# Another order at attention's end, w_out's chunks loaded ahead, and other steps for the evictions and the refill of the first down projection

## The reference

```python
h = rms_norm(x, norm_mix)
q, k, v, cb, cc, cu = split(h @ w_in)          # 8 heads of 64; 512 conv channels
q, k = rms_norm(q, q_norm), rms_norm(k, k_norm)     # per head
z = q @ k.T / 8                                # s < t only
a = sigmoid(z) * prod(1 - sigmoid(z_tj) for s < j < t)
attn = a @ v
conv = cb * conv3(cc * cu)                     # causal, depthwise
x = x + concat(attn, conv) @ w_out
h = rms_norm(x, norm_ffn)
x = x + (silu(h @ w_gate) * (h @ w_up)) @ w_down    # d_ff 2816
```

## Time and profile before

| | |
|---|---|
| median of 3 runs | 2509.22 us |
| the profiled execution | 2507.85 us, of which 2506.0 span |
| PE busy | 2435.7 us (97%), DVE 57%, POOL 53%, ACT 47% |
| 330 to 1005 us, attention | PE busy 660.52 of 675 |
| 1005 to 1055 us, its end and mix's opening | PE busy 36.56 of 50, mean clock 0.90 |
| 1055 to 1210 us, rest of mix | PE busy 155.00 of 155 |
| 1210 to 1650 us, gate and up, first half | PE busy 436.78 of 440 |
| 1650 to 1868 us, down, first half | PE busy 209.27 of 218 |
| 1868 to 2285 us, gate and up, second half | PE busy 414.51 of 417 |
| 2285 to 2506 us, down, second half | PE busy 214.74 of 221 |

### The profile page before, as it was taken

One profiled execution on the slowest core, in us unless ns is written; L12 is line 12 of the kernel. 1 busy time (PEld: TensorE's weight loads), 2 busy tenths in 40 slices (PEclk: granted clock), 3 DMA queues, 4 the chain that ended last, 5 costly groups with the idle time before them and its releaser, 6 DMA issues.

```text
span 2506.0 us, 34829 instructions
## 1 busy us (share of the span) xinstructions
PE 2435.7 (97%) x12008; PEld 2031.9 (81%) x12008; DVE 1417.4 (57%) x1461; ACT 1168.2 (47%) x1864; POOL 1324.2 (53%) x918
## 2 busy tenths in 40 slices
PE   8999989999899999799999999999999999999999
PEld 6788878888788888688788888878778888888887
DVE  4444367777777777435665555535645555553343
ACT  3322267777777777323433333334443333333433
POOL 1455367778678687203655445324875455451253
PEclk9999999999999999999999999999999999999999
DMA  5989855443534532444432332467553322325766
GB/s 185 300 287 289 270 173 126 135 109 99 159 96 113 149 100 73 134 143 168 143 115 87 113 103 92 152 225 249 184 187 101 121 90 98 126 76 188 227 208 203
DMA packets 337225, 388.17 MB, mean 155 GB/s; under 512 B 21440, under 2 KB 242752, under 8 KB 334784
## 3 DMA queue, kind: packets, MB, share of 16 engines
q1 hardware_dynamic: 337088, 386.49, 49.1%
HBM read 263.20 MB, written 123.21 MB: 154 GB/s over the span
## 4 chain that ended last, share of the span: by engine, by line
PE 87%; POOL 3%; DVE 3%; DMA 2%; issue 2%; SPq 1%; ACT 1%; DVEq 0%; ACTq 0%; POOLq 0%
PE lay_ps L2447 11%; PE lay_ps L2449 11%; PE lay_ps L2451 11%; PE lay_ps L102 9%; PE lay_ps L103 9%; PE lay_ps L104 9%; PE lay_ps L2477 5%; PE lay_ps L2479 4%; PE lay_ps L2478 4%; PE lay_ps L1281 4%; PE lay_ps L1288 2%; PE lay_ps L1265 2%; PE lay_ps L1287 2%; PE lay_ps L1266 2%; POOL lay_A L2356 1%
## 5 line engine op out<-in xcount | busy, mean ns | idle before, releaser
L2356 POOL TENSOR_TENSOR lay_A<-lay_raw,lay_A 128x512 fp32r<-128x512 f32 x264 | 364.3, 1392 | 378.5 <-ACT lay_A L1988 378.5
L2447 PE MATMUL lay_ps<-lay_B,lay_A 128*128 128x512 f32 x1232 | 480.0, 390 | 2.7 <-ACT lay_s L2010 2.7
L2451 PE MATMUL lay_ps<-lay_B,lay_A 128*128 128x512 f32 x1232 | 479.5, 389 | 0.0
L2449 PE MATMUL lay_ps<-lay_B,lay_A 128*128 128x512 f32 x1232 | 479.5, 389 | 0.0
L1132 DVE TENSOR_TENSOR_SCAN lay_stick<-lay_ps,lay_stick 128x128 f32<-128x128 f32 (+5 forms) x192 | 331.2, 1725 | 146.7 <-ACT lay_ps L1033 136.1
L1185 POOL TENSOR_TENSOR lay_a<-lay_a,lay_stick 128x128 f32<-128x128 f32 (+5 forms) x192 | 281.4, 1471 | 144.1 <-DVE lay_stick L1132 137.5
L1988 ACT ACTIVATE lay_A<-lay_raw 128x512 fp32r<-128x512 f32 x264 | 162.2, 627 | 300.0 <-DMA lay_raw<-in_w_gate 119.6
L2032 ACT ACTIVATE lay_A<-lay_A_over 128x1024 fp32r<-128x1024 f32 x154 | 163.1, 1060 | 251.9 <-PE lay_ps L2479 225.9
L2223 DVE TENSOR_TENSOR lay_A<-lay_A_over,lay_A 128x1024 fp32r<-128x1024 f32 x104 | 155.1, 1494 | 211.1 <-ACT lay_A L2032 211.0
L2447 PEld LDWEIGHTS lay_ps<-lay_B,lay_A 128*128 128x128 f32 x1232 | 231.5, 188 | 51.6 <-POOL lay_A L2356 2.9
L2449 PEld LDWEIGHTS lay_ps<-lay_B,lay_A 128*128 128x128 f32 x1232 | 231.5, 188 | 48.0
(11 more groups left out here) (143 smaller groups left out, 5033.0 us busy)
## 6 DMA issues: line engine op xcount, KB each, us to landing
hid_ops<-lay_s SPq DMA_DIRECT2D x154, 256.0 KB, 2.1
lay_A_over<-hid_ops SPq DMA_DIRECT2D x154, 256.0 KB, 3.0
lay_w_stage<-in_w_in SPq DMA_DIRECT2D x48, 512.0 KB, 4.9
lay_raw<-in_w_gate SPq DMA_DIRECT2D x22, 1024.0 KB, 5.7
lay_raw<-in_w_up SPq DMA_DIRECT2D x22, 1024.0 KB, 8.1
lay_A_over<-wd_ops SPq DMA_DIRECT2D x88, 256.0 KB, 3.6
lay_A_over<-in_w_down SPq DMA_DIRECT2D x66, 256.0 KB, 4.1
lay_wd_raw<-in_w_down SPq DMA_DIRECT2D x11, 1024.0 KB, 6.7
```

The lines of the kernel that those rows point to most:

```text
L2356: nc.gpsimd.tensor_tensor(A[:, j, p, 1, :, :], operand(j, p), A[:, j, p, 0, :, :].bitcast(F32), ALU.subtract).then_inc(lo_done, 1)
L2447: nc.tensor.matmul(ps[:, b, :], A[:, j, p, 0, k, :], B[p][:, 0, k, :], start=first_mm, stop=False, skip_group_check=True)
L2449: nc.tensor.matmul(ps[:, b, :], A[:, j, p, 0, k, :], B[p][:, 1, k, :], start=False, stop=False, skip_group_check=True)
L2451: mm = nc.tensor.matmul(ps[:, b, :], A[:, j, p, 1, k, :], B[p][:, 0, k, :], start=False, stop=last_mm, skip_group_check=True)
```

## The change

At attention's end the units' last pieces, mix's splits, the weights' splits and the chunks stand in another order on ACT, DVE and PE. DVE takes over POOL's two splits of the first tiles, and its scan of unit 47 stands behind the low part of unit 44. Six chunks of w_out are loaded ahead instead of two; chunks c = 2 to 5 have buffers of their own in the part of `aT` that no group uses. The order of chunks becomes 0, 1, 2, 4, 6, 3, 7, 5 for tiles 0 and 1.

In the down projection the two halves share the new places of evictions, of `y_to_21` and `y_to_22`, of `store_z` 0 and `load_z` 1, and the new order of raw buffers (with it the four first loads wait for product 6). In the first half `load_b` issues two per step at e = 10 to 17, and the b pieces have other steps. At the second half's start ACT makes casts 2 to 7 before its round and 8 to 13 inside it, each with the wait that it needs.

```diff
+        mix["w_early"] = []
+        for part in ("aT_hi", "aT_lo"):
+            m.offset = m.starts[part] + 4 * GW * (KB + KB // 2)
+            mix["w_early"] += [m.at(f"m_w_early_{part}{i}", [P, D]) for i in range(2)]
...
             store_o(PAIRS - 1, NG - 3)
-            mix["load_w"](2)
-            mix["load_w"](3)
+            mix["load_w"](6)
+            mix["load_w"](7)
...
             pairs(act, body)
-            for i in range(2):
-                mix["mix_split"](i)
-            for n in range(NU - LAG, NU):
-                aT_part(PAIRS - 1, n)
-                if opens[n - 1]:
-                    o_part(PAIRS - 1, units[n - 1][0] - 1)
-                mix["w_part"](n - NU + LAG)
+            mix["mix_split"](0)
+            aT_part(PAIRS - 1, NU - 3)
+            mix["w_part"](0)
+            mix["mix_split"](1)
+            aT_part(PAIRS - 1, NU - 2)
+            o_part(PAIRS - 1, NG - 2)
+            aT_part(PAIRS - 1, NU - 1)
+            mix["w_part"](1)
+            mix["w_part"](2)
             o_part(PAIRS - 1, NG - 1)
...
-                    running_product(p, n)
+                    late = is_last(p) and n == NU - 1
+                    if not late:
+                        running_product(p, n)
...
                         aT_part(p, n - LAG)
+                    if late:
+                        running_product(p, n)
 
             pairs(dve, body)
-            for n in range(NU - LAG, NU):
-                aT_part(PAIRS - 1, n)
-                if opens[n - 1]:
-                    o_part(PAIRS - 1, units[n - 1][0] - 1)
-                if n > NU - LAG:
-                    mix["w_part"](n - NU + LAG - 1)
+            aT_part(PAIRS - 1, NU - 3)
+            mix["mix_split"](0)
+            mix["w_part"](0)
+            mix["mix_split"](1)
+            aT_part(PAIRS - 1, NU - 2)
+            aT_part(PAIRS - 1, NU - 1)
+            o_part(PAIRS - 1, NG - 2)
+            mix["w_part"](1)
             o_part(PAIRS - 1, NG - 1)
...
             pairs(pool, body)
-            for i in range(2):
-                mix["first_split"](i)
...
             pairs(pe, body)
-            for n in range(NU - LAG, NU):
-                if opens[n]:
-                    upper_values(PAIRS - 1, units[n][0] - 1)
-                transposes(PAIRS - 1, n)
-                if opens[n]:
-                    lower_values(PAIRS - 1, units[n][0] - 1)
-                if n > NU - LAG:
-                    for i in range(2):
-                        mix["chunk"](i, n - NU + LAG - 1)
+            transposes(PAIRS - 1, NU - 3)
+            upper_values(PAIRS - 1, NG - 2)
+            transposes(PAIRS - 1, NU - 2)
+            lower_values(PAIRS - 1, NG - 2)
+            transposes(PAIRS - 1, NU - 1)
+            for i in range(2):
+                mix["chunk"](i, 0)
             lower_values(PAIRS - 1, NG - 1)
+            for i in range(2):
+                mix["chunk"](i, 1)
...
+    CHUNKS = (0, 1, 2, 4, 6, 3, 7, 5)
...
-        def load_w(k):
-            wait(sp, w_lo_done, k - 1)
-            sp.dma_start(w_stage[:, k % 2, :], w_out[k * P:(k + 1) * P, :]).then_inc(w_in_sem[k % 2], DMA)
+        def load_w(c):
+            k = CHUNKS[c]
+            if c > 5:
+                sp.wait_ge(w_lo_done, c - 5)
+            sp.dma_start(w_raw(c), w_out[k * P:(k + 1) * P, :]).then_inc(w_loaded(c), DMA)
...
             sp.wait_ge(att.z_full, att.first_head_scored)
-            load_w(0)
-            load_w(1)
+            for c in range(6):
+                load_w(c)
...
-T_AT, B_HI_AT, B_LO_AT = 26, 31, 34
+T_AT = (19, 21, 23, 25, 27, 29, 31, 37, 39, 41, 43, 45, 51, 53, 55, 57)
+B_HI_AT, B_LO_AT = (27, 39, 48, 59), (28, 40, 58, 66)
...
-        op_raw = [flat(Af, j, p) for j, p in ((GATE, P5), (GATE, P6), (UP, P5), (UP, P6))]
+        op_raw = [flat(Af, j, p) for j, p in ((UP, P6), (GATE, P5), (GATE, P6), (UP, P5))]
...
-        hi_at, lo_at = ([first + 7 * m // 5 for m in range(28)] for first in (B_HI_AT, B_LO_AT))
+        hi_at = [first + 9 * i // 7 for first in B_HI_AT for i in range(7)]
+        lo_at = [first + 9 * i // 7 for first in B_LO_AT for i in range(7)]
...
-                    if G == 0 and e - 10 in range(4 * GT):
-                        load_b(e - 10)
-                    if e == ENDS[D2] + 10:
+                    if G == 0 and e - 10 in range(2 * GT):
+                        load_b(2 * (e - 10))
+                        load_b(2 * (e - 10) + 1)
+                    if e == ENDS[D2] + 13:
                         store_z(G, 0)
-                    if e == ENDS[D2] + 13:
+                    if e == ENDS[D2] + 15:
                         load_z(G, 1)
...
                     if p in (P5, P6):
-                        act.wait_ge(dve_lo, ON_DVE * G)
-                        act.wait_ge(pool_lo, ON_POOL * G)
+                        wait_lo(act, G - 1, STEPS - RAWS + ((GATE, P5), (GATE, P6), (UP, P5), (UP, P6)).index((j, p)))
+                    elif (j, p) in ((UP, P2), (UP, P4)):
+                        act.wait_ge(tile_done, GT * (STEPS * G - 2))
+                    elif (j, p) in ((GATE, P7), (GATE, P2)):
+                        act.wait_ge(tile_done, GT * (STEPS * G - 1))
...
                     keep(R, GATE, 0)
+                    if c == 0:
+                        hi(R, 8)
+                        hi(R, 9)
                     keep(R, UP, 0)
-                    if more:
+                    if c == 0:
+                        hi(R, 10)
+                        hi(R, 11)
+                    if more and c:
                         hi(R + 1, 0)
                     keep(R, GATE, 1)
+                    if c == 0:
+                        hi(R, 12)
+                        hi(R, 13)
+                        hi(R + 1, 0)
                     if more:
                         hi(R + 1, 1)
                     if ahead:
...
+                    if e == STEPS - 2 and G + 1 < HALVES:
+                        hi(ROUNDS * (G + 1), 2)
                 if G + 1 < HALVES:
-                    for n in range(2, NP):
+                    for n in range(3, 8):
                         hi(ROUNDS * (G + 1), n)
...
-                    for d, evict in ((D2, evict_11), (D6, evict_w), (D7, evict_y), (D4, evict_21), (D5, evict_22)):
+                    for d, evict in ((D6, evict_w), (D5, evict_22)):
                         if e == ENDS[d] + OPS:
                             for t in range(GT):
                                 evict(G, t)
                     if e % 3 < 2:
                         op_lo(G, e)
-                    if G == 0 and e - T_AT in range(16):
-                        t_piece(e - T_AT)
+                    for d, evict, after in ((D2, evict_11, 3), (D7, evict_y, 3)):
+                        if e - ENDS[d] - after in range(GT):
+                            evict(G, e - ENDS[d] - after)
+                    if e - ENDS[D4] - OPS in range(2):
+                        for t in range(2):
+                            evict_21(G, 2 * (e - ENDS[D4] - OPS) + t)
+                    if G == 0 and e in T_AT:
+                        t_piece(T_AT.index(e))
...
-                    for at, add in ((39, x2_to_w), (51, y_to_21), (ENDS[D5] + 4, y_to_22)):
+                    for at, add in ((39, x2_to_w), (50, y_to_21), (ENDS[D5] + 5, y_to_22)):
```

More of the change, by code:

```diff
@@ L1410, in mix_stage @@
     TAIL = TILES - 2
-    assert len(ORDER) == TILES
+    CHUNKS = (0, 1, 2, 4, 6, 3, 7, 5)
+    assert len(ORDER) == TILES and len(CHUNKS) == KT
     def spare(i, shape, **sizes):
@@ L1419, in mix_stage @@
     mix_t, h_out = spare(B22, "p (b k t) -> p b k t", k=KT), spare(T4, "p (b k t) -> p b k t", k=KT)
-    first_t, first_hi, first_lo, mix_hi, mix_lo, w_stage, w_hi, w_lo, gain, xn, ss, msq, rstd = (
-        lay[n] for n in ("first_t", "first_hi", "first_lo", "mix_hi", "mix_lo", "w_stage", "w_hi", "w_lo", "gain", "xn",
-                         "ss", "msq", "rstd"))
+    first_t, first_hi, first_lo, mix_hi, mix_lo, w_stage, w_early, w_hi, w_lo, gain, xn, ss, msq, rstd = (
+        lay[n] for n in ("first_t", "first_hi", "first_lo", "mix_hi", "mix_lo", "w_stage", "w_early", "w_hi", "w_lo", "gain",
+                         "xn", "ss", "msq", "rstd"))
     tr = ps[:, 2:4, :].rearrange("p b (j t) -> p b j t", t=P)
@@ L1426, in mix_stage @@
     x_in, x2_stored = [m.sem("x_in0"), m.sem("x_in1")], [m.sem("x2_stored0"), m.sem("x2_stored1")]
-    w_in_sem, h2_stored = [m.sem("w_in0"), m.sem("w_in1")], [m.sem("h2_stored0"), m.sem("h2_stored1")]
+    w_in_sem, w_early_in = [m.sem("w_in0"), m.sem("w_in1")], [m.sem(f"w_early_in{i}") for i in range(4)]
+    h2_stored = [m.sem("h2_stored0"), m.sem("h2_stored1")]
     w_hi_done, w_lo_done, mix_hi_done, mix_lo_done = (
@@ L1547, in mix_split, with w_part @@
             nc.scalar.activation(hi_of(i), raw_of(i), ACT.Copy).then_inc(mix_hi_done, 1)
-        def w_part(k):
-            act.wait_ge(w_in_sem[k % 2], DMA * (k // 2 + 1))
+        def w_part(c):
+            k = CHUNKS[c]
```

(23 more changed lines are left out.)

31 lines of the change are left out of this document (15 added, 16 removed).

## The result

| | before | changed |
|---|---|---|
| median of 4 runs each, side by side | 2508.93 us | 2490.60 us (2487.55 to 2493.21) |
| ratio, 95% interval | | 0.9925 [0.9912, 0.9937] |
| the profiled execution | 2507.85 us, span 2506.0 | 2487.55 us, span 2485.8 |

The forecast was 2492 (2485 to 2499). A second set of four runs of the changed kernel gave 2490.76 and 0.9930 [0.9913, 0.9946].

What follows compares the result with a forecast made beforehand. PE's waits, and half clock after them, were taken as the bound. Terms -16.5 + 2.5 - 0.6 - 0.6 - 3.7 + 1.9 = -17.0 turned 2507.85 into 2490.9; the median lies 1.4 higher: 2492 us, range 2485 to 2499.

Steps and rivals of the forecast that it cites:

- Opening, -16.5: Attention's end to mix's tile 2: reordering, DVE's splits in a row and earlier w_out loads save 16.5 us.
- Rival (b): Opening gives 3 to 5 us less, through further clock falls or shared-port delays of DVE's splits: about 2496; chance 0.14.
- Loads, +2.5: First down projection, steps 10 to 17: two b loads per step saturate the DMA and delay operands, costing 2.5 us.
- Rival (c): The crowded loads cost their full lag, +6 us instead of +2.5: 2495.5; chance 0.12.
- rival (d): SP itself is held back by slow issues in steps 10 to 17: +25 us, 2514.5 in all; chance 0.03.
- `evict_w`, -0.6: First down projection, step 33: without a `t_piece` ahead on DVE, the wait falls from 1.0 to about 0.4 us.
- Step 42, -0.6, and step 44, 0: First down projection: the smaller 0.4 us wait goes, saving 0.6; PE's 2.2 us wait for POOL at 44 stays.
- Steps 53 to 58, -3.7: First down projection: waits from `evict_21` blocking DVE go, with restarts 3.7 us less; `y_to_21` is late next.
- Costed at nothing: Edits put at 0 us, among them the four first operand loads waiting for product 6 instead of 3.
- Refill, +1.9: Second half's start: product 3's wait goes, but late raw columns stall products 8 and 9: net 1.9 us more.
- Rival (a): Raw's reload in the refill is not late, so its waits go: 4.6 us less, 2487.5; chance 0.22.
- rival (e): Loads ahead collide with attention, which loses what the opening gains: 2508.7 us; chance 0.02.

Runs made afterwards that it cites:

- experiment 1: Kernel before with only the opening's edits, its down projection unchanged: 2493.21 us against 2510.70, ratio 0.9927.
- experiment 8: Changed kernel with DVE's four b subtractions of steps 39, 41, 43, 45 moved to steps 46 to 49: 2491.05 us, 0.9934 of the kernel before.
- experiment 9: Changed kernel with all 28 low parts of the b operands made by DVE instead of POOL, a few steps earlier: 2487.84 us, 0.9916 of the kernel before.

## Why the prediction was right, step by step

- **Opening, -16.5: measured -17.1.** T(45) came 1.0 earlier (1.1 forecast), chunk (0,0) 6.15 behind it (6.1), tile 2 28.5 behind it (29). That DVE makes the splits in a row was the right reason: with two of the three given back to POOL the opening cost 3.2 more. The fall of the clock that "may stay" did not here; in experiment 1, with the same opening, it did and cost 0.3, not the 1.2 that I had allowed. The wait that I had put before chunk (0,1) did not come. Rival (b), an opening that gives less, fell.
- **Loads, +2.5: right in place and size.** `keep_x` and step 17 together wait 2.5 where it was 0.4; spreading the loads took 2.6 off the phase, 1.9 of it in these two waits. Rival (c), 6, was too dear. Of rival (d) the first half came (single issues of 0.72 to 1.51 and one of 2.32, had one of 1.71), but not on all four of a step: SP's four issues come at the pace of the transfers, 3.16 on the mean.
- **`evict_w`, -0.6: wrong, +0.2.** The step reads "no `t_piece` stands ahead of it on DVE now; the wait of 1.0 falls to about 0.4". The `t_piece` is gone, but DVE's split of step 34, which also stands ahead, met two of POOL's b pieces that the new steps put there and took 1.99 instead of 1.23. 1.05 - 0.6 + 0.76 is the 1.21 that was measured. I had applied the contention of DVE and POOL at step 44 and not ten steps earlier. DVE, then POOL:

```profile
1719.12 1.99 DVE L2259 TENSOR_TENSOR lay_A<-lay_A_over,lay_A 128x1024 fp32r<-128x1024 f32 x1 [1.50 <-ACT lay_A L2056]
1721.04 2.47 DVE L2275 TENSOR_TENSOR lay_s<-lay_ps,lay_s 128x512 f32<-128x512 f32 x4
...
1716.47 3.56 POOL L2425 TENSOR_TENSOR lay_B<-lay_B_over,lay_B 128x512 fp32r<-128x512 f32 x2
```

- **Step 42, -0.6, and step 44, 0: right.** The 0.4 is gone with its restart; the wait at 44 is 2.07 where it was 2.19. Spacing the pieces within the stretch saved nothing, taking some out of it did (experiments 8 and 9).
- **Steps 53 to 58, -3.7: -2.7 in waits, some -3.3 with restarts.** `evict_21` delays nobody. The 0.2 that is left at step 53 is `y_to_21` waiting for z, named as what is late next; in experiment 8 it grew to 2.6.
- **Costed at nothing.** The first four operand loads: PE's waits at steps 4 and 5 fell from 0.9 to 0.3, which I didn't have. It is no gain of these loads as far as the runs show: in experiment 1, which has the loads of before, the two waits are 0.4, and in the nine other runs with the changed loads 0 to 0.8. The phase came out at -2.4, as summed, partly by luck: this 0.6 and the miss of 0.8 at `evict_w` cancel, and the two other profiles of the same phase without a fall of the clock would have made it -2.1 and -3.1.
- **Refill, +1.9: measured +1.1.** The wait at product 3 is gone, and those at products 8 and 9 are 2.1 and 1.3 (2.8 and 1.4 forecast), with the raw load issued 13.6 us after the last step (13 forecast). The size was off because raw UP landed 7.4 after its issue, not 8.1 as before, which the sum had carried over. Rival (a), no late reload, fell.
- Nothing is seen of rival (e): attention is not longer, and PE waits nowhere from 930 to 1002 us, where the four further loads might have made it wait. -17.0 was the sum, -17.1 - 2.4 + 1.1 = -18.4 the stages, and -18.3 the medians.

## What to carry to other kernels

When instructions of an engine that works in order are moved to make something earlier, list what it now waits for ahead of a copy that PE needs: the refill gave its gain back because copies of finished products stood behind casts of data that were still loading. Two causes of one wait (a load too late and an order too late) add up here, 7 and 8 of 17, and a wait list blames the same instruction for both; the row of the cast ahead of it tells them apart. Every subtraction with two operands in SBUF on DVE is counted against POOL's and the other way round, step by step, not only where a wait already shows.
